# Choice of tokens sorted inside the output projection, first expert's weights loaded there, and six smaller moves in a two-layer trunk

## The reference, cut to what matters

```python
def trunk_layer(...):
    mix, mix_c = mixer(h, hc, ctx_out)               # ends with  ... @ w_out
    x = x + gt1 * rmsnorm(mix, g_post_mix)
    h = rmsnorm(x, g_pre_ffn) * (1 + sc2) + sh2
    x = x + gt2 * rmsnorm(expert_choice_ffn(h, ...), g_post_ffn)
    # layer 0 does the same for the context, layer 1 does not

def expert_choice_ffn(h, w_router, w_gate, w_up, w_down):
    cap = CAPACITY_FACTOR * n // N_EXPERTS           # 128 of 1024 tokens, 32 of 256
    aff = softmax(h @ w_router)
    gate, idx = lax.top_k(swapaxes(aff, 1, 2), cap)
    xg = h[idx]
    hid = silu(xg @ w_gate) * (xg @ w_up)
    out = (hid @ w_down) * gate[..., None]
    return zeros_like(h).at[idx].add(out)
```

## Time and profile before

| | |
|---|---|
| median of 3 executions | 3768.49 us (3767.53 to 3776.51) |
| the profiled execution, its own time | 3772.22 us |
| its span, first to last instruction | 3770.5 us |
| mean granted TensorE clock | 0.944 of full speed |
| PE busy | 3357.1 us, 89% |
| DVE, ACT, POOL busy | 1178.4, 955.1, 502.7 us |
| moved by DMA | 675.50 MB |

### The profile page before, as it was taken

One profiled execution on the slowest core, in us unless ns is written; L12 is line 12 of the kernel. 1 busy time (PEld: TensorE's weight loads), 2 busy tenths in 40 slices (PEclk: granted clock), 3 DMA queues, 4 the chain that ended last, 5 costly groups with the idle time before them and its releaser, 6 DMA issues. The chain is left out here.

```text
span 3770.5 us, 53381 instructions
## 1 busy us (share of the span) xinstructions
PE 3357.1 (89%) x20560; PEld 2493.6 (66%) x20560; DVE 1178.4 (31%) x2901; ACT 955.1 (25%) x2175; POOL 502.7 (13%) x655
## 2 busy tenths in 40 slices
PE   6999889969996599999999689898889489999995
PEld 4888645546553587788778565565665277888874
DVE  3212367556523301110111144555662510100112
ACT  3111256635432001110111132244442111111111
POOL 0000232110000011001100240245000000000002
PEclk8999999989998799999999889999899699999997
DMA  6336445443133677787778630101312579988886
GB/s 209 117 104 127 136 161 170 138 133 96 44 111 115 244 250 255 255 272 250 252 255 274 191 130 0 51 19 41 82 33 98 186 251 321 320 304 314 314 315 225
DMA packets 381859, 675.50 MB, mean 179 GB/s; under 512 B 80720, under 2 KB 119808, under 8 KB 375488
## 3 DMA queue, kind: packets, MB, share of 16 engines
q1 hardware_dynamic: 345408, 544.22, 42.3%
q10 hardware_dynamic: 22864, 82.59, 6.1%
q0 software_dynamic: 13440, 46.80, 5.1%
HBM read 587.38 MB, written 92.36 MB: 180 GB/s over the span
## 5 line engine op out<-in xcount | busy, mean ns | idle before, releaser
L2226 PE MATMUL experts_gu_ps<-experts_xT,experts_wg 128*128 128x160 f32 (+1 forms) x4096 | 552.8, 289 | 4.6 <-DVE experts_xT L2154 2.6
L2226 PE MATMUL experts_gu_ps<-experts_xT,experts_wu 128*128 128x160 f32 (+1 forms) x4096 | 550.2, 288 | 0.0
L2226 PEld LDWEIGHTS experts_gu_ps<-experts_xT,experts_wg 128*128 128x128 f32 x4096 | 529.7, 192 | 19.4 <-issue 19.4
L2226 PEld LDWEIGHTS experts_gu_ps<-experts_xT,experts_wu 128*128 128x128 f32 x4096 | 525.8, 192 | 0.0
L2196 PE MATMUL experts_y_ps<-experts_wd,experts_hid 128*128 128x512 f32 x1024 | 452.3, 597 | 0.0
L2167 DVE TENSOR_TENSOR experts_hid<-experts_sil,experts_gu_ps 128x160 f32<-128x160 f32 (+1 forms) x256 | 77.9, 304 | 942.6 <-ACT experts_sil L2131 942.6
L2131 ACT ACTIVATE experts_sil<-experts_gu_ps 128x160 f32<-128x160 f32 (+1 forms) x256 | 74.3, 290 | 1107.9 <-PE experts_gu_ps L2226 1107.9
L2196 PEld LDWEIGHTS experts_y_ps<-experts_wd,experts_hid 128*128 128x128 f32 x1024 | 190.8, 190 | 231.1 <-issue 228.3
L2103 POOL DMA_INDIRECT moe<-experts_y,experts_ixs x32 | 51.2, 1600 | 1130.8 <-DVE experts_y L2171 1130.8
L2171 DVE TENSOR_SCALAR experts_y<-experts_y_ps,experts_wt 128x512 f32<-128x512 f32 x32 | 24.0, 751 | 449.4 <-PE experts_y_ps L2196 449.4
L2526 PE MATMUL front_pb_ps<-kept_hT,front_ahead_w 128*128 128x512 f32 (+1 forms) x384 | 138.7, 522 | 0.7 <-DVE kept_dt L2578 0.7
(11 more groups left out here) (421 smaller groups left out, 4745.9 us busy)
## 6 DMA issues: line engine op xcount, KB each, us to landing
experts_wg<-in_l_w_gate SPq DMA_DIRECT2D x64, 2048.0 KB, 8.5
experts_wu<-in_l_w_up SPq DMA_DIRECT2D x64, 2048.0 KB, 12.8
experts_wd<-in_l_w_down SPq DMA_DIRECT2D x64, 2048.0 KB, 11.1
attn_a_mod_w<-in_l_w_mod ACTq DMA_DIRECT2D x36, 1024.0 KB, 4.9
proj<-proj_ob ACTq DMA_DIRECT2D x60, 256.0 KB, 2.3
proj_ahead_w<-in_l_w_in SPq DMA_DIRECT2D x6, 2048.0 KB, 9.5
attn_near_bias<-lines SPq DMA_DIRECT2D x80, 128.0 KB, 2.8
mix_xr<-res SPq DMA_DIRECT2D x18, 512.0 KB, 4.2
```

What stands on the lines that cost most here:

```text
L2226: mm = nc.tensor.matmul(GU[f % 2][:, part, 0:N], w[:, h, k, c * P:(c + 1) * P], xT[:, k, :], start=(k == 0), stop=(k == KD - 1))
```

## The change

Seven edits.

1. The affinities stay in SBUF. `tail` copies them into `work`, now three tensors of 16 partitions: tokens 0 to 639, 640 to 1023, and the context. Their rounds are no longer done side by side but one group after another; some are placed inside `tail` of tiles 5 and later, the rest (`rounds_after`) at the head of `experts`. The tensor `affinity`, its stores, the clear and the loads go.
2. The six loads of the first expert's weights are issued by SP in `mix_out`, one after each `load_residual`. The zero writes now follow the sort.
3. Head 1's q and k are loaded after one load of modulation weights, and `prepare` waits for q's or k's rotation alone. The bias additions of the modulation (L302) are spread between other DVE work.
4. The last head is normalised and stored in two parts, eight tiles and two.
5. Near attention takes the context tiles first; half of the first bias table is issued by ACT, half by SP, and its v before it.
6. The last two fills of the scan change places, so that the last rotation is in the loop.
7. The last turn of POOL's expert loop stands behind the loop, and SP, not POOL, waits for the last scatter.

```diff
 # mix_out, SP
                 for n in range(2, tiles):
                     load(n)
                     load_residual(n)
+                    if n - 2 < 6:
+                        following.load_first(sp, n - 2)
 # mix_out, ACT
-                    act.wait_ge(af_done, START + n + 1)
-                    act.dma_start(affinity[:, at], af[:, slot, :]).then_inc(a_out[slot], 16)
 # mix_out, DVE: tail(n)
                     nc.vector.tensor_tensor(xr[:, slot, :], tmp[:], xr[:, slot, :], ALU.add).then_inc(x_done, 1)
+                    sort(n, 0)
                     dve.wait_ge(tx_done, START + n + 1)
...
                     v.then_inc(hv, 1)
+                    sort(n, 1)
                     dve.wait_ge(l_done, START + n + 1)
...
-                    nc.vector.tensor_copy(af[:, slot, :], A[0:E, P:2 * P]).then_inc(af_done, 1)
+                    nc.vector.tensor_copy(choice.place_of(n), A[0:E, P:2 * P]).then_inc(af_done, 1)
 # class Choice
+    def rounds_in(self, n):                      # (group, first, end), ahead of the two waits of tail(n)
+        if n == NTX:
+            return ((0, 15, 16), (1, 0, 3)), ((1, 3, 4),)
+        if n == NTX + 1:
+            return ((1, 4, 7),), ((1, 7, 9),)
+        if 5 <= n:
+            return ((0, 5 * (n - 5), 5 * (n - 5) + 3),), ((0, 5 * (n - 5) + 3, 5 * (n - 5) + 5),)
+        return (), ()
+    def rounds_after(self):
+        return ((1, 9, 16), (2, 0, 4)) if self.with_ctx else ((0, 15, 16), (1, 0, 16))
+    def round(self, link, group, j):
+        link(vector.max(val, work))
+        link(vector.max_index(idx, val, work))
+        if j + 1 < self.ROUNDS[group]:
+            link(vector.match_replace(work, val, work, -1.0))
 # experts, SP
-                choice.load(sp)
-                load_weights(0)
                 with sp.Fori(0, E - 1) as e:
                     load_weights(e + 1)
                 following.load(sp)
+                sp.wait_ge(s_done, E * IX)
 # experts, DVE
-                choice.begin(dve, link)
+                choice.select(dve, link)
                 dve.wait_ge(vec_in, START + 16 * (2 * conds + 1))
...
-                choice.select(dve, link)
+                choice.merge(dve, link)
 # experts, POOL
-                with pool.Fori(0, E) as e:
+                with pool.Fori(0, E - 1) as e:
                     link.turn(e, 6 if with_ctx else 3)
                     chosen(e)
                     gather(e + 1)
+                    scatter(e)
                     pool.wait_ge(s_done, e * IX + IX)
+                link.over(E - 1)
+                chosen(E - 1)
+                gather(E)
                 pool.wait_ge(g_done, (E + 1) * IX)
+                scatter(E - 1)
 # differential_attention
                 load_v(0)
-                for n in range(later.SLOTS):
+                later.load(sp, 0)
+                load_qk(1)
+                for n in range(1, later.SLOTS):
                     later.load(sp, n)
-                load_qk(1)
...
-                        pe.wait_ge(rope_done, START + 2 * h + 2)
+                        pe.wait_ge(rope_done, START + 2 * h + 1 + which)
...
-                normalise(H - 1)
+                normalise(H - 1, 0, NT - 2)
+                normalise(H - 1, NT - 2, NT)
 # local_attention, near
+    def tile(n):
+        return (n + NTX) % NQ if near else n % NQ
-                    for h2, cls, a in PARTS:
+                    bias_parts(sp, i, PARTS if i else PARTS[:len(PARTS) // 2])
+                if near:                         # at the head of ACT's stream
+                    bias_parts(act, 0, PARTS[len(PARTS) // 2:])
 # scan
-    FILLS = [... for j, t in enumerate(Z_ORDER[:7]) for fill in (("q", j), ("z", t))] + [("z", Z_ORDER[7]), ("q", 7)]
+    FILLS = [fill for j, t in enumerate(Z_ORDER) for fill in (("q", j), ("z", t))]
...
-                rotate(NTX - 1)
                 root(NTX - 1)
```

More of the change, by code:

```diff
@@ L300, in add_bias @@
             dve.wait_ge(self.bias_in, START + 16 * GROUPS * len(self.rest))
-        for j in range(GROUPS):
-            self.nc.vector.tensor_tensor(self.rows[strip(j), a, :], self.acc[strip(j), :], self.bias[strip(j), a, :], ALU.add).then_inc(self.added, 1)
+        self.nc.vector.tensor_tensor(self.rows[strip(j), a, :], self.acc[strip(j), :], self.bias[strip(j), a, :], ALU.add).then_inc(self.added, 1)
     def store(self, sp):
@@ L1388, in exp @@
                 def exp(n, m):
-                    s, (first, end) = n % SLOTS, span(n % NQ)
+                    s, (first, end) = n % SLOTS, span(tile(n))
                     act.wait_ge(copied[m], START + chunk_at[n + 1])
@@ L1417, in _ @@
                         exp(ahead, waiting.pop(0))
-                    for j in range(len(rounds(n % NQ))):
+                    for j in range(len(rounds(tile(n)))):
                         if (turn_at[n] + j) % 2 == 0:
@@ L1475, in _ @@
                 for n in range(AHEAD):
-                    for j in range(len(chunks(n % NQ))):
+                    if near and n == NTC:
+                        outside(dve, link, nc.vector, 0)
+                    for j in range(len(chunks(tile(n)))):
                         scores(n, j, 0)
@@ L1481, in _ @@
                     ahead = n + AHEAD
-                    todo = list(range(len(chunks(ahead % NQ)))) if ahead < ITEMS else []
-                    mine = [j for j in range(len(rounds(n % NQ))) if (turn_at[n] + j) % 2 == 1]
+                    todo = list(range(len(chunks(tile(ahead))))) if ahead < ITEMS else []
+                    mine = [j for j in range(len(rounds(tile(n)))) if (turn_at[n] + j) % 2 == 1]
                     if n >= 1:
@@ L1568, in _ @@
                     ahead = n + AHEAD
-                    todo = list(range(len(chunks(ahead % NQ)))) if ahead < ITEMS else []
-                    turns = len(rounds(n % NQ))
+                    todo = list(range(len(chunks(tile(ahead))))) if ahead < ITEMS else []
+                    turns = len(rounds(tile(n)))
                     for j in todo:
@@ L1581, in _, with mix_out @@
                     weigh_values(n, turns - 1)
-def mix_out(nc, name, K, first, tiles, mixed, mod, g_post, g_pre, res, normed, affinity):
+def mix_out(nc, name, K, first, tiles, mixed, mod, g_post, g_pre, res, normed, choice, following):
     HALF = KD // 2
@@ L1718, in turned_rows, with sort @@
                     nc.vector.tensor_copy(oT[:, n % 2], TO[:]).then_inc(o_out, 1)
+                def sort(n, place):
+                    for group, first, end in choice.rounds_in(n)[place]:
+                        for j in range(first, end):
+                            if j == 0:
+                                dve.wait_ge(af_done, START + (5, NTX)[group])
+                            choice.round(link, group, j)
                 def tail(n):
```

259 lines of the change are left out of this document (132 added, 127 removed).

## The result

| | before | after |
|---|---|---|
| time, median of 13 runs each | 3767.53 us (3762.87 to 3776.51) | 3777.06 us (3773.47 to 3784.63) |
| ratio after / before, 95% interval | | 1.0025 (1.0016 to 1.0033) |
| profiled execution, its span | 3772.2, 3770.5 us | 3774.8, 3773.1 us |

The changed kernel is slower by 9.5 us. The prediction said no change, and 3767. So I take totals from the medians, and from the traces only stretches.

The account below looks back on a forecast made before the run. PE was taken as the bound nearly everywhere, idling about 400 us at stage boundaries. Terms -12 - 14 + 15 - 5.7 + 22 - 7 = -2 gave 3770 from 3772.2, or 3767 as median; own range 3756 to 3778, eight in ten 3730 to 3790.

Parts of the forecast that it names:

- the projections with their choices: Both layers' projections and token choices, with sort, weights and clock: +15 us in layer 0, +22 in layer 1.
- the weights: Projections: 2 MB loads ahead of `mix_ot` on SP's queue make PE wait 2.6 us in five tiles, +13 a layer.
- the sort: Token choice: boundaries save 26.8 and 11.1 us; rounds in tiles cost 18.5 and 9.8, last tiles 0.5 and 3.3.
- Edit 5: Start of near attention: two-queue issue brings the first score with a table at 9.7 us, -5.7; context tiles first, -5.
- the context tiles first: Near attention: PE works on the context tiles while DVE fills the pipeline with full tiles, -5 us.
- Edit 6: End of the scan: the last rotation moves into the loop, ahead of a y POOL waits for anyway, -5.7 us.
- Edit 7: End of the experts: less POOL idling before the next stage, -7 us for both layers, bounds 0 and -7.5.
- Edit 3: Attention A: both waits for rotated q go, and slow clock behind the first, -12 us, bounds -8 and -14.
- Edit 4: End of attention A: only a fifth of the normalising passes and store follows the last tile, -3.5 us.
- clock cost: Projections: PE's clock falls after new waits, 0.9 us for each of ten; overall 10 us in layer 0, 7 in layer 1.
- The rival of 3789: Projections: the clock falls at each of twenty new waits, 3 us each in place of 1, +22; chance 0.15.
- The first rival: Projections: small loads are not late, so 26 us of waits and 9 of clock fall away, 3732; chance 0.37.

Follow-up runs that it names:

- f4: e1 with all 20 loads of near attention's first bias table issued by SP alone; 3748.0 us, 0.9941 of the kernel before.
- g1: e1 with near attention as in the kernel before; 3747.2 us, 0.9942 of the kernel before.
- f3: e1 with the scan's rotation of tile 7 one step earlier; 3739.9 us, 0.9924 of the kernel before.
- f1: e1 with POOL's last expert turn in the loop again and POOL waiting for the scatter; 3745.6 us, 0.9932 of the kernel before.
- e3: Kernel before with edits 3 to 7 alone, its affinities, sort and weights kept; 3750.0 us, 0.9957 of the kernel before.
- e1: Changed kernel with the first expert's weights issued by SP at the head of experts, not in the projection; 3748.7 us, 0.9956 of the kernel before.
- e2: Changed kernel with the six weight loads issued by ACT behind the softmax exponential; 3748.8 us, 0.9956 of the kernel before.
- g4: Changed kernel with SP's weight load put ahead of load_residual instead of behind it; 3746.9 us, 0.9945 of the kernel before.

## Why the prediction was wrong, by its own steps

The sum was -39 for edits 3 to 7 and +37 for the projections with their choices. It came out as -16 and +27. Two large terms were to cancel; the first was wrong by 23 us and the second by 10. That 3767 lies only 10 us beside the measured 3777 is luck: the weights and the sort were priced too high as well.

**Edit 5, the first step that failed** ("Two queues issue ten each in 6.4 us, behind v: first score with the table at 9.7 us, -5.7"). The issue went as said, but the table did not come:

```profile
753.23 6.53 ACTq L1290 DMA_DIRECT2D attn_near_bias<-lines  x10
...
753.66 6.42 SPq L1290 DMA_DIRECT2D attn_near_bias<-lines  x10
...
769.31 0.69 DVE L1466 CUSTOM_DVE_ANT_0 attn_near_e<-attn_near_s_ps,attn_near_bias 128x512 f32<-128x512 f32 x1 [8.35 <-DMA attn_near_bias<-lines]
```

The first score has its table 16.0 us after the start, against 15.4 before. The windows tell why. Before, while SP issued the twenty loads (stretch, its length, five engines' busy time, PE's clock, share of the DMA engines, GB/s):

```profile
773.00:776.00 3.00, 0.00 (x0) 0.00 (x0) 0.00 (x0) 0.00 (x0) 1.91 (x7) 0.50 0.72 199
776.00:779.00 3.00, 0.00 (x0) 0.00 (x0) 0.00 (x0) 0.00 (x0) 0.00 (x0) 0.50 0.71 208
```

and after, with two queues:

```profile
762.00:765.00 3.00, 0.00 (x0) 0.00 (x0) 0.00 (x0) 0.00 (x0) 0.00 (x0) 0.50 1.07 244
765.00:768.00 3.00, 0.00 (x0) 0.00 (x0) 0.00 (x0) 0.00 (x0) 0.00 (x0) 0.50 1.08 239
```

A load of the table has 128 KB, and SP issues one in 0.64 us: 205 GB/s, with the engines at 0.7 of their time. Two queues fill the engines at 240. Twenty loads are 2.6 MB and v 0.66, which is 13.7 us at that rate (an estimate from these windows), and in the first 2 us the rate is 80 only; one queue or two, the table is there after 16 us (f4). I had priced the issue and never the bytes, though the size is a row of the profile. The other half, the context tiles first (-5), came to 3 at most: the first product with v is 4.6 us earlier (22.7 us after the start, 27.3 before), but near takes 243.7 to 246.2 and not 246.5 (g1). That what ends near is the chain that starts with the table fits this, and isn't shown. In all edit 5 gave between 0.6 and 2.5 us for 10.7.

**Edit 6** ("In the loop it lies in front of a y that POOL waits for anyway"). The scan of the changed kernel takes 260.7 us and 258.6 to 261.7 in those that share its order: 0 in place of -5.7. The rotation moved from behind the last y to in front of it, with that y already there (f3). I had looked at what it left and not at when POOL is free where it arrives: its preceding work ends at 2612.46, 0.4 us after y.

**Edit 7** ("I take -7, as the straight stream of attn_a is the nearest row"). 2 us in layer 0 and nothing in layer 1 (f1). The 9.4 us of idle time were 3.3 us until the scatter had landed and 6.1 of the stage's end, of which the loop is 2.0.

**Edit 3** was priced at 12. Attention A ends 9.0 us earlier in the trace of after, and between 5.2 and 12.1 in the others, with a mean of 9.0 over all thirteen kernels that have it: inside the bounds of 8 to 14, 3 short of the term. One or two of these three are PE's wait for DVE ahead of attention's first turned tile (L1003): 1.5 us before, 2.4 to 3.4 in the thirteen. No run takes the order of these loads out alone, so the third stays open. **Edit 4** at -3.5 measured -4.5 (14.4 to 9.9, the same in all). So the stretches give 9 + 4.5 + 1.5 + 0 + 2 = 17 us for edits 3 to 7, as e3's 16 has it, and what is missing is 9 us of edit 5, 6 of edit 6, 5 of edit 7 and 3 of edit 3.

**The weights** were right in mechanism: first in, first out, and five waits a layer. The new waits for `mix_ot` are 31.4 - 7.8 = 23.6 us for 26 predicted. Their clock cost is 1.7 us after each of the two longest, 3.41 and 3.48, and none after the other eight (0.67 to 3.26 us), where I took 0.9 for each: 3.4 us in place of 9. With it the weights cost 28 to 30 us (e1, e2, g4; 26 to 30 by the ratios) where I had 35. The Trainium skill ("DMA: Bandwidth & Descriptors", section "Queues, rings and completion order") has it that on each DMA engine the ring of one issuer is taken in order while the rings of other issuers take turns; e2 agrees, with 4.1 us for a landing that took 8.8. The rival of 3789 wanted 3 us at each new wait; that holds for none of them, and it falls. The Trainium skill ("TensorE: Matmul & The Clock Gate", section "HAM oscillation — how this bites in real kernels") tells of a kernel in which each tile starts cold behind a DMA wait, and the waits that it gives there are all longer than the 2.6 us priced here. The trace agrees with it in the waits of 3.41 and 3.48 us and in none of the shorter ones (0.67 to 3.26), so the prediction should not have read it as a rule for every stall.

**The sort** was right within its size: rounds of 2.68 and 1.88 us, a layer-0 gap of 20.1 us at `turn` and 32.7 in layer 1 (18 and 32 by the sum), tiles of 23.0 to 24.8 us in e1 for 23.4 without the clock. In all it is worth 1 us: what it takes off the boundary it puts on the tiles.

The first rival, small loads in time, did not come true by itself; e1 and g4 made it so: 28 to 30 us better, where I had 35.

## What to carry to other kernels

Before a load is issued from a second queue, multiply its bytes: where one queue already moves 205 of the 240 GB/s, a second brings little (here nothing with v ahead, 1 to 2 us with v behind). When a step is moved off the end of a stage, look at where it arrives as closely as at where it left; it gains only if its engine is idle there longer than the step is long. And a large load that is to be hidden in a loop goes in front of the issue that waits anyway, not in front of the one that the bottleneck engine reads next: here two exchanged lines were 30 us.

## What was not expected of the hardware

The price of a wait beyond itself is not smooth: in neighbouring tiles 2.12 us of wait left six products at 2.74 us, and 3.41 us made them 4.44, while 3.26 us in layer 1 cost nothing more. And a table in pieces of 128 KB moved at 240 GB/s with the engines' share at 1.07, while the 2 MB loads of weights, in the projection, reach 328 at 0.93 (this window of the changed kernel, 1045.9 to 1052.0 us):

```profile
1045.90:1052.00 6.10, 5.92 (x28) 3.47 (x27) 2.12 (x8) 2.51 (x7) 0.00 (x0) 1.00 0.93 328
```

So the rate at which the engines were full was not the same for both kinds of load here, and a load's bytes are to be divided by the last column of a window of its own kind, not by the largest rate seen in the kernel.
